# Moving the constants and staging tiles of a float32 trunk kernel in on-chip memory, and starting the shared region at a multiple of 256 bytes

## The chip, the core and the metric

The kernel runs on one core of a Trainium2 chip. The metric is the device time of one execution in microseconds (us). Before the change three runs took 2451.73, 2452.22 and 2452.22 us (median 2452.22). One more execution was profiled: it took 2452.22 us, of which its trace covers 2450.5 us from the first to the last instruction; the remaining 1.7 us lie around the trace.

The engines are TensorE (PE in the profile, its weight loads PEld), VectorE (DVE), ScalarE (ACT), GpSimd (POOL) and SyncE (SP), which here only issues DMAs. On-chip memory (SBUF) has 128 partitions; a tile has the same byte address in each, and "address" below always means that byte address.

## The reference, cut to what matters

A model trunk with 256 tokens and width 2048, all in float32. Layer 0 mixes tokens by retention and RWKV-7, layer 1 by a convolution and a gated linear recurrence; after each comes a squared-ReLU MLP of width 8192, and a final norm ends it.

```python
h = h + even_mixer(rmsnorm(h, ev_norm))            # in: 2048 x 7456, out: 2048 x 2048
h = h + relu(rmsnorm(h, ff_norm[0]) @ ff_w1[0])**2 @ ff_w2[0]   # 2048 x 8192, 8192 x 2048
h = h + odd_mixer(rmsnorm(h, od_norm))             # in: 2048 x 4096, out: 2048 x 2048
h = h + relu(rmsnorm(h, ff_norm[1]) @ ff_w1[1])**2 @ ff_w2[1]
out = rmsnorm(h, final_norm)
```

## The kernel before, in words

**Weights as a stream.** Every large matrix product is cut into groups of 512 output columns (one has 288) and each group into 8 units of 256 rows of the weight matrix. A unit is one DMA of 512 KB into a slot of the ring `raw` (4 slots, issued by SP in `load_unit`). ACT copies it to the rounded form `w_hi` (L189), DVE writes the remainder `w_lo` = `raw` - `w_hi` (L194), and PE multiplies the unit with the activations, which are split in the same way: for each block of 128 rows and each half of the tokens it forms hi x hi, hi x lo and lo x hi (L205 to L207). In these matmuls the 128x128 block of activations is the loaded weight of the array, and 512 columns of `w_hi` or `w_lo` stream past it. There are 95 groups, of which 94 have 512 columns.

**Activations.** The left factor is `xT_hi`, `xT_lo` for products that read the normed input, and `hidA_hi`, `hidA_lo`, `hidB_hi`, `hidB_lo` (together "hid") for the products that read a hidden activation: half of each MLP and both output projections. After a group, ACT takes the result to the staging tile `stg` (L270), POOL squares it in the MLPs (L278), PE transposes it with the identity in `con` (L302), and ACT and DVE split it into hid. Groups of residual columns are added to `x` by DVE (L352).

**RWKV.** Between 180 and 585 us the kernel runs the RWKV recurrence in 8 passes: small float32 matmuls of 128x128 blocks (all issued by the helper at L688) on tiles named `key_bd`, `beta_bd`, `level_a`, `inv_t` and the like, into whose gaps the matmuls of the retention projection are woven.

**What sets the order.** Every engine has its program in a fixed, hand-written order, and semaphores by count tie them together. Nothing in it reads an address to choose an order.

**Memory.** One slab from address 16512 holds everything. `Region` is a bump allocator over it: each call gives the next bytes, rounded up to 32. `lasting` holds what lives through the kernel. A shared region begins at `low`; in it the tiles of RWKV, retention, the odd layer and hid lie over one another, since they live at different times. Before, `lasting` was in two parts: `x`, `xT_hi`, `xT_lo`, `raw`, `w_hi`, `w_lo` ahead of the shared region, then 93568 bytes of shared region, then `par` (gains and biases), `con` (identity, ones, masks), `ssq`, `rstd`, `lam`, `stg` and `junk` behind it.

Of the kernel before, what the change touches and what calls it, by code (L numbers as in the profile page):

```python
# [11 lines left out]
P = 128  # L12
T = 256
HALVES = T // P
D = 2048
KT = D // P
# [34 lines left out]
def trunk(nc, x_in, params, consts, cossin, rdecay, ev_w_in, ev_w_out, rw_w2, rw_a2, rw_g2, od_w_in, gx_w, ga_w,  # L51
          od_w_out, ff_w1, ff_w2, final_norm, out):
    ctx = ExitStack()
    with ctx:
# [17 lines left out]
        slab_start = -(-nc.sbuf_base // 32) * 32  # L72
# [13 lines left out]
        lasting = Region(0)  # L86
# [3 lines left out]
        raw = lasting("raw", [P, RING, KU, WIDE])  # L90
        w_hi = lasting("w_hi", [P, RING, KU, WIDE], F32R)
        w_lo = lasting("w_lo", [P, RING, KU, WIDE], F32R)
        HALF = KT // 2 * T * 4
        low, shared_end = lasting.at, lasting.at + 93568

        lasting = Region(shared_end)
        par = lasting("par", [P, NPAR])
        con = lasting("con", [P, NCONST])
        ssq = lasting("ssq", [P, 4, HALVES])
# [2 lines left out]
        stg = lasting("stg", [P, 2, HALVES, WIDE])  # L102
        junk = lasting("junk", [P, WIDE])
        ident = con[:, CIDENT:CIDENT + P]

        at_a = Region(low)
        hidA_hi, hidA_lo = (at_a(n, [P, KT // 2, T], F32R) for n in ("hidA_hi", "hidA_lo"))
        at_b = Region(low + 4 * HALF)
        hidB_hi, hidB_lo = (at_b(n, [P, KT // 2, T], F32R) for n in ("hidB_hi", "hidB_lo"))
# [32 lines left out]
        gate_a = od_a("gate_a", [P, KT, T])  # L142
        od_b = Region(low + 4 * HALF)
        gate_x = od_b("gate_x", [P, KT, T])
        x_rest = Region(low + 2 * HALF)
        conv = x_rest("conv", [P, KT, T])
# [1633 lines left out]
```

## Time and profile before

| | |
|---|---|
| profiled execution | 2452.22 us |
| its span in the trace | 2450.5 us |
| PE busy | 2403.4 us, 98% of the span |
| PE weight loads busy | 2021.8 us, 83% |
| DVE busy | 1407.3 us, 57% |
| ACT busy | 1133.0 us, 46% |
| POOL busy | 240.3 us, 10% |
| DMA | 411.21 MB, 168 GB/s over the span |
| mean granted PE clock | 0.996 of full speed |

An engine is busy while it carries out an instruction; overlapping matmuls count once. Matmuls are pipelined, so the distance from one start to the next tells more than the duration of one.

### The profile page before, as it was taken

The numbers are of one execution on the slowest core, as the hardware profiler recorded it, in microseconds if no ns is written. First come the engines' busy times: TensorE is split into PE (matmuls) and PEld (weight loads), VectorE is DVE, ScalarE is ACT, GpSimd is POOL, SyncE is SP. The second block draws the span as 40 slices with busy tenths as digits, with TensorE's granted clock in tenths as the row PEclk, the third lists the DMA queues.
The fourth block names the chain that finished last, engine by engine and source line by source line (L and its number), as shares of the span: only waits on it lengthen the run. The fifth ranks groups of instructions, "written<-read, shape, count | busy, mean of one in ns | idle before, by whom it ended". The sixth has DMA issues, their size and how long they took to land.

```text
span 2450.5 us, 32124 instructions
## 1 busy us (share of the span) xinstructions
PE 2403.4 (98%) x11710; PEld 2021.8 (83%) x11710; DVE 1407.3 (57%) x1613; ACT 1133.0 (46%) x1459; POOL 240.3 (10%) x184
## 2 busy tenths in 40 slices
PE   7999999999999999999999999989999999999998
PEld 6878888888788888888888888878888888888886
DVE  5467777775555555545555566775555554555554
ACT  5454444444444444344344545765443443443443
POOL 0001123342000000000000000230000000000001
PEclk9999999999999999999999999999999999999999
DMA  7652223333565666565666565545666656656654
GB/s 219 189 147 84 83 86 88 88 87 97 166 186 180 197 190 186 192 189 182 196 183 192 184 201 177 175 147 186 181 192 194 189 182 196 185 187 196 188 186 158
DMA packets 215432, 411.21 MB, mean 168 GB/s; under 512 B 13264, under 2 KB 19792, under 8 KB 215184
## 3 DMA queue, kind: packets, MB, share of 16 engines
q1 hardware_dynamic: 213888, 407.01, 54.5%
q0 software_dynamic: 1424, 2.49, 0.4%
q8 instruction: 89, 1.46, 0.3%
q14 instruction: 31, 0.25, 0.0%
HBM read 407.35 MB, written 2.10 MB: 167 GB/s over the span
## 4 chain that ended last, share of the span: by engine, by line
PE 87%; DVE 2%; ACT 2%; issue 1%; POOL 0%; ACTq 0%; DVEq 0%; POOLq 0%
PE acc L205 25%; PE acc L207 25%; PE acc L206 25%; PE tp L688 6%; PE tp L302 2%; PE acc L688 1%; PE acc L1490 1%; PE tp L1490 1%; DVE stg L635 1%; ACT w_hi L189 0%; ACT L680 0%; DVE w_lo L194 0%; DVE state L858 0%; DVE gate_t L1553 0%; DVE stg L636 0%
## 5 line engine op out<-in xcount | busy, mean ns | idle before, releaser
L194 DVE TENSOR_TENSOR w_lo<-raw,w_hi 128x1024 fp32r<-128x1024 f32 (+1 forms) x760 | 987.1, 1304 | 891.9 <-ACT w_hi L189 890.2
L189 ACT ACTIVATE w_hi<-raw 128x1024 fp32r<-128x1024 f32 (+1 forms) x760 | 800.4, 1056 | 945.3 <-PE acc L207 933.7
L205 PE MATMUL acc<-w_hi,xT_hi 128*128 128x512 f32 (+1 forms) x1760 | 706.1, 401 | 6.5 <-DVE w_lo L194 4.3
L207 PE MATMUL acc<-w_hi,xT_lo 128*128 128x512 f32 (+1 forms) x1760 | 684.4, 389 | 0.0
L206 PE MATMUL acc<-w_lo,xT_hi 128*128 128x512 f32 (+1 forms) x1760 | 683.5, 388 | 0.0
L205 PEld LDWEIGHTS acc<-w_hi,xT_hi 128*128 128x128 f32 x1760 | 332.1, 189 | 69.0 <-DVE w_lo L194 3.8
L207 PEld LDWEIGHTS acc<-w_hi,xT_lo 128*128 128x128 f32 x1760 | 331.2, 188 | 68.7
L206 PEld LDWEIGHTS acc<-w_lo,xT_hi 128*128 128x128 f32 x1760 | 332.1, 189 | 60.5
L205 PE MATMUL acc<-w_hi,hidA_hi 128*128 128x512 f32 x640 | 252.8, 395 | 6.3 <-DVE hidA_lo L1524 6.3
L206 PE MATMUL acc<-w_lo,hidA_hi 128*128 128x512 f32 x640 | 251.1, 392 | 0.0
L207 PE MATMUL acc<-w_hi,hidA_lo 128*128 128x512 f32 x640 | 250.9, 392 | 0.0
L205 PE MATMUL acc<-w_hi,hidB_hi 128*128 128x512 f32 x640 | 250.6, 392 | 0.0
L207 PE MATMUL acc<-w_hi,hidB_lo 128*128 128x512 f32 x640 | 249.1, 389 | 0.0
L206 PE MATMUL acc<-w_lo,hidB_hi 128*128 128x512 f32 x640 | 249.0, 389 | 0.0
L278 POOL TENSOR_TENSOR stg<-stg 128x1024 f32<-128x1024 f32 x32 | 60.6, 1895 | 1358.3 <-ACT stg L270 1358.3
L205 PEld LDWEIGHTS acc<-w_hi,hidA_hi 128*128 128x128 f32 x640 | 121.5, 190 | 31.6 <-issue 6.7
L207 PEld LDWEIGHTS acc<-w_hi,hidA_lo 128*128 128x128 f32 x640 | 121.3, 190 | 25.5
L206 PEld LDWEIGHTS acc<-w_lo,hidA_hi 128*128 128x128 f32 x640 | 121.5, 190 | 24.8
L207 PEld LDWEIGHTS acc<-w_hi,hidB_lo 128*128 128x128 f32 x640 | 120.1, 188 | 25.0
L205 PEld LDWEIGHTS acc<-w_hi,hidB_hi 128*128 128x128 f32 x640 | 120.1, 188 | 24.7
L206 PEld LDWEIGHTS acc<-w_lo,hidB_hi 128*128 128x128 f32 x640 | 120.2, 188 | 24.7
L270 ACT ACTIVATE stg<-acc,rstd 128x512 f32<-128x512 f32 (+1 forms) x94 | 59.2, 681 | 68.1 <-PE acc L207 67.8
(230 smaller groups left out, 1731.1 us busy)
## 6 DMA issues: line engine op xcount, KB each, us to landing
raw<-in_ff_w SPq DMA_DIRECT2D x512, 512.0 KB, 3.7
raw<-in_ev_w_in SPq DMA_DIRECT2D x112, 512.0 KB, 3.6
raw<-in_od_w_in SPq DMA_DIRECT2D x64, 512.0 KB, 4.1
raw<-in_ev_w_out SPq DMA_DIRECT2D x32, 512.0 KB, 3.8
raw<-in_od_w_out SPq DMA_DIRECT2D x32, 512.0 KB, 3.8
raw<-in_ev_w_in SPq DMA_DIRECT2D x8, 288.0 KB, 5.3
x<-in_x_in SPq DMA_DIRECT2D x4, 512.0 KB, 6.6
gate_w<-in_gx_w SPq DMA_DIRECT2D x8, 256.0 KB, 2.8
```

The costliest lines, as they stand in the source:

```text
L189: act.activation(w_hi[:, j % RING, :, 0:wide], raw[:, j % RING, :, 0:wide], ACT.Copy).then_inc(hi_ready, 1)
L194: dve.tensor_tensor(w_lo[:, j % RING, :, 0:wide], raw[:, j % RING, :, 0:wide], w_hi[:, j % RING, :, 0:wide], ALU.subtract).then_inc(lo_rea ...
L205: nc.tensor.matmul(o, hi[:, tok], wh, start=(kt == 0), stop=False)
L206: nc.tensor.matmul(o, hi[:, tok], wl, start=False, stop=False)
L207: last = nc.tensor.matmul(o, lo[:, tok], wh, start=False, stop=(kt == KT - 1))
L270: last = act.activation(stg[:, g["bank"], h, 0:g["wide"]], acc[2 * g["bank"] + h][:, 0:g["wide"]], g.get("func", ACT.Relu if g["post"] == ...
L278: pool.tensor_tensor(s, s, s, ALU.mult).then_inc(squared, 1)
L302: last = nc.tensor.transpose(tp[2 * b + c // 2][0:s.shape[1], (c % 2) * T + h * P:(c % 2) * T + (h + 1) * P], s, ident)
L635: own(dve.reciprocal(nrm_t, nrm_t))
L688: return nc.tensor.matmul(out, lhsT, rhs, start=first, stop=last)
L1490: last = nc.tensor.matmul(odd_gate_banks(v, n)[i][:, jh * T:(jh + 1) * T], gate_w[:, n % 2, i, ih, jh * P:(jh + 1) * P], conv[:, 2 * n + i ...
```

## The change

The seven tiles `par` to `junk` are allocated right behind `w_lo`, without a gap, and the shared region begins behind them, at the next address that is a multiple of 256. All tiles keep their shapes and their order within their region.

```diff
         w_lo = lasting("w_lo", [P, RING, KU, WIDE], F32R)
-        HALF = KT // 2 * T * 4
-        low, shared_end = lasting.at, lasting.at + 93568
-
-        lasting = Region(shared_end)
         par = lasting("par", [P, NPAR])
         con = lasting("con", [P, NCONST])
...
         junk = lasting("junk", [P, WIDE])
         ident = con[:, CIDENT:CIDENT + P]
-
+        HALF = KT // 2 * T * 4
+
+
+        low = lasting.at + -(slab_start + lasting.at) % (2 * P)
         at_a = Region(low)
```

The addresses that follow, and what is left of each when it is divided by 256:

| tile | before | rest | after | rest |
|---|---|---|---|---|
| `x` | 16512 | 128 | 16512 | 128 |
| `xT_hi`, `xT_lo` | 32896, 49280 | 128 | the same | 128 |
| `raw`, `w_hi`, `w_lo` | 65664, 82048, 98432 | 128 | the same | 128 |
| `par` | 208384 | 0 | 114816 | 128 |
| `con` | 209504 | 96 | 115936 | 224 |
| `stg` | 215840 | 32 | 122272 | 160 |
| `junk` | 224032 | 32 | 130464 | 160 |
| shared region, `hidA_hi`, `gate_a` | 114816 | 128 | 132608 | 0 |
| `hidB_hi`, `z` | 147584 | 128 | 165376 | 0 |
| `v_bd` to `seen_v` (RWKV), `qT` | from 177856 | 192 | from 195648 | 64 |
| `gate_w` | 180544 | 192 | 198336 | 64 |

The seven tiles move down by 93568 bytes and the shared region up by 17792; both are odd multiples of 128, so what is left on division by 128 is the same for every tile. Each engine has the same instructions, with the same shapes and the same waits, in the same order; only addresses in them differ. All line numbers from `HALF` on are lower by up to 4 (those of the engines' work by 1).

## Rows read from the trace of the kernel before

**Rows 1.** The page: span, busy time, granted clock.
```profile
span 2450.5 us, 32124 instructions
PE 2403.4 (98%) x11710; PEld 2021.8 (83%) x11710; DVE 1407.3 (57%) x1613; ACT 1133.0 (46%) x1459; POOL 240.3 (10%) x184
PEclk9999999999999999999999999999999999999999
```

**Rows 2.** The page: the chain that ended last, by engine.
```profile
PE 87%; DVE 2%; ACT 2%; issue 1%; POOL 0%; ACTq 0%; DVEq 0%; POOLq 0%
```

**Rows 3.** Waits of PE, longest first: total us, times, longest.
```profile
PE tp L302 <- DMA par<-in_params: 6.5, 1, 6.5
PE acc L205 <- DVE hidA_lo L1524: 6.3, 1, 6.3
PE tp L1298 <- POOL qT L1203: 4.4, 2, 2.8
PE acc L205 <- DVE w_lo L194: 4.3, 2, 3.4
...
PE tp L688 <- ACT rhs_u L917: 1.5, 7, 0.2
```

**Rows 4.** The last chain by time, 2438 to 2451 us: start, us, what.
```profile
2438.55 0.24 PE acc L207
...
2443.87 1.22 ACT x L1694 x2
```

**Rows 5.** Timeline near 1000 us, left factor hid: start, duration, instruction.
```profile
999.72 0.39 PE L206 MATMUL acc<-w_lo,hidA_hi 128*128 128x512 f32 x1
...
999.95 0.19 PEld L205 LDWEIGHTS acc<-w_hi,hidA_hi 128*128 128x128 f32 x1
...
1000.37 1.06 ACT L189 ACTIVATE w_hi<-raw 128x1024 fp32r<-128x1024 f32 x1 [1.66 <-PE acc L207]
1000.40 0.39 PE L206 MATMUL acc<-w_lo,hidA_hi 128*128 128x512 f32 x1
...
1003.35 0.39 PE L207 MATMUL acc<-w_hi,hidB_lo 128*128 128x512 f32 x1
```

**Rows 6.** Timeline near 1105 us, left factor xT, POOL squaring `stg`.
```profile
1103.93 0.39 PE L205 MATMUL acc<-w_hi,xT_hi 128*128 128x512 f32 x1
...
1104.20 1.90 POOL L278 TENSOR_TENSOR stg<-stg 128x1024 f32<-128x1024 f32 x1 [21.62 <-ACT stg L270]
...
1105.10 2.07 DVE L194 TENSOR_TENSOR w_lo<-raw,w_hi 128x1024 fp32r<-128x1024 f32 x1 [2.73 <-ACT w_hi L189]
...
1105.97 0.39 PE L205 MATMUL acc<-w_hi,xT_hi 128*128 128x512 f32 x1
```

**Rows 7.** Groups by line and shape: busy us, mean ns, idle before.
```profile
L302 PE MATMUL tp<-con,stg 128*128 128x128 f32 x372 | 48.2, 272 | 1.3 <-ACT stg L270 1.3
...
L688 PE MATMUL tp<-beta_bd,key_bd 128*128 128x128 f32 x320 | 42.1, 274 | 0.0
```

**Rows 8.** One line, the convolution taps: duration min, median, max in ns.
```profile
L1471 DVE SCALAR_TENSOR_TENSOR conv<-x_raw,par,conv x48: 473/480/2628, 1456.9 to 1558.2; 128x256 f32<-128x256 f32 x48
```

**Rows 9.** The page: hid as left factor, staging and squaring.
```profile
L206 PE MATMUL acc<-w_lo,hidA_hi 128*128 128x512 f32 x640 | 251.1, 392 | 0.0
L205 PE MATMUL acc<-w_hi,hidB_hi 128*128 128x512 f32 x640 | 250.6, 392 | 0.0
...
L278 POOL TENSOR_TENSOR stg<-stg 128x1024 f32<-128x1024 f32 x32 | 60.6, 1895 | 1358.3 <-ACT stg L270 1358.3
...
L270 ACT ACTIVATE stg<-acc,rstd 128x512 f32<-128x512 f32 (+1 forms) x94 | 59.2, 681 | 68.1 <-PE acc L207 67.8
```

**Rows 10.** DMA issues: count, KB each, median us from issue to landing.
```profile
raw<-in_ff_w SPq DMA_DIRECT2D x512, 512.0 KB, 3.7
...
stg<-in_final_norm SPq DMA_DIRECT2D x1, 1024.0 KB, 6.5
...
par<-in_params SPq DMA_DIRECT2D x1, 137.5 KB, 4.7
```

## The prediction

> **What bounds the kernel now.** I read the totals first, then the chain that ended last, then who PE waited for, and then timelines at two places. The totals show PE busy for 2403.4 of 2450.5 us, at full granted clock in every slice, and no other engine above 57% [rows 1]. So PE sets the time, and 47.1 us are left in which it does nothing. The chain of waits says the same: 87% of it is PE, and the issue gaps, DVE and ACT have 1 to 2% each [rows 2]. Of the 47.1 us, 11.7 come after the last matmul (it ends at 2438.8 us, and the span at 2450.5 [rows 1, 4]) and 6.5 at the very start, where PE waits for the load of `par`; the other 28.9 us are short waits in between, the longest 6.3 us [rows 3].
>
> "PE busy" could still hide slack, because matmuls overlap. The timelines show the real step. Where the left factor is hid, 16 steps take from 999.72 to 1003.35 us, that is 226.9 ns each [rows 5]. Where it is xT, 9 steps take from 1103.93 to 1105.97 us, 226.7 ns each [rows 6]. The 512 columns of one matmul at the upper clock level, 2.4 GHz, need 213.3 ns, so PE is within 13.6 ns of its own floor at each step. A weight load takes 190 ns [rows 5] and fits under the step.
>
> **The change, part by part.** Nothing is added, removed or reordered on any queue; the waits are the same, and so are the DMAs and their sizes. What can cost or save time is the address alone, and only these parts of it change: bit 7 and the bits above. I take the groups of operands in turn.
>
> *The stream of weights.* `raw`, `w_hi`, `w_lo`, `x` and the xT tiles keep their addresses. So all 760 weight loads from memory, ACT's rounding, DVE's remainder and the columns that stream through PE are as before, as are both factors in 55 of the 95 groups. Cost 0.
>
> *Hid as the weight of the array.* This is the largest part that moves: six groups of 640 matmuls (two of them in [rows 9]), 3840 in all, whose left factor starts on a rest of 0 in place of 128 after division by 256. No tile that PE reads in the kernel before starts on a multiple of 256, so the trace has no such matmul, and I bound it. Upper bound of a gain: all 13.6 ns over the column time go, 3840 x 13.6 = 52 us. Upper bound of a loss: the same 13.6 ns more, 52 us. The value that I take is 0, by the nearest rows. First, xT at 32896 and hid at 114816 and 147584 lie far apart and step alike within 0.2 ns [rows 5, 6]. Second, two kinds of small float32 matmul have operands on different rests: the transposes of `stg` with `con` (32 and 96) come to 48.2 / 372 = 130 ns each, and the RWKV products of `beta_bd` and `key_bd` (both 192) to 42.1 / 320 = 132 ns [rows 7]. Third, what moves is the side that is loaded, and at 190 of 227 ns a faster load would not be seen.
>
> *RWKV, retention, odd-layer and `stg` operands of ACT, DVE and POOL.* The convolution taps are the best test in the trace: the rows of `x_raw` are 1036 bytes long and the taps are shifted by 4 bytes, so the 48 instructions start on rests from 128 upward and round past 0 to 60. Their minimum is 473 and their median 480 ns; the maximum of 2628 ns belongs to an instruction that met POOL [rows 8]. A start address that shifts by single words is not seen there. I take 0. As for the bound, these engines reach the end only through PE's 28.9 us of middle waits: if all their moved work became 10% cheaper or dearer, the waits would shrink or grow by about 2.9 us. The tail of 11.7 us has `stg` (final gains) and `junk` in it, and 10% of that is 1.2 us, which I fold into the same bound.
>
> *DMA.* The transfers into moved tiles are single ones (`par`, `con`, the masks, the final gains) or lie under other work; the stream into `raw`, which holds 407 of 411 MB with its neighbours, stays. The only moved transfer that PE visibly waits for is `par`: 4.7 us from issue to landing, 6.5 us of PE wait [rows 3, 10]. I take 0, and 10% of its 4.7 us, 0.5 us, as the bound in either direction.
>
> The Trainium skill speaks against the change here ("DMA: Bandwidth & Descriptors", section "How a descriptor splits into AXI transactions"): a descriptor is cut at 256-byte boundaries, and a start off such a boundary still pays for the bytes below it. `par` goes from a rest of 0 to 128. By that rule its 1100 bytes per partition cost 39 beats of 32 bytes in place of 35; estimated from the page, with the 4.7 us of this trace, that is +0.5 us. No row of the kernel before shows the two starts side by side. The sum above doesn't use it.
>
> **Sum.** 2450.5 us of span + 1.7 us around it + 0 + 0 + 0 + 0 = 2452.2 us. The profiled execution took exactly the median of the three runs, so nothing has to be carried over.
>
> **The rivals.** The measurement can tell a change of about 0.2%, 4.9 us, from none; I use that as the border below.
>
> *A, faster: aligned weights shorten PE's step.* The 13.6 ns over the column time could be the price of handing over to a weight block whose 512-byte rows straddle three 256-byte pieces in place of two. Then the 3840 hid matmuls would each save up to 13.6 ns: 2452.2 - 52 = 2400 us; from 1.3 ns per step on, it would pass the border. For it: the overhead is there and is constant, as a fixed cost would be. Against it: the weight load is hidden, and the small matmuls with rests of 32 and 96 against 192 and 192 show no difference worth the name.
>
> *B, slower: `stg` and `con` now lie directly behind `w_lo`.* If the memory had blocks in which one engine's access holds up another's, PE reading `w_lo` would now collide with ACT writing `stg` (59.2 us in all) and POOL squaring it (60.6 us) [rows 9]. A slowdown of PE by 10% over these 119.8 us gives +12 us, 2464 us; it decides from 4.1% on (4.9 / 119.8). Against it: in [rows 5] ACT writes one slot of `w_hi` while PE reads another slot of the same tile, 4 to 12 KB away, closer than `stg` will be to most of `w_lo`, and PE keeps its 227 ns. In [rows 6] POOL squares `stg` and doubles a DVE subtraction to 2.07 us, and PE still steps by 226.7 ns. The Trainium skill ("SBUF — State Buffer", section "Who interferes with whom") says that only the port pair shared by VectorE and GpSimd causes contention; the trace agrees in these two places, and by it B is worth nothing, and the time stays at 2452.2 us.
>
> *C, small shifts of phase.* If some DVE or ACT work in RWKV or the retention part were touched, the 28.9 us of waits would move: 2449 to 2455 us. That is inside the border for nearly every size I can give it, so I count it with the forecast.
>
> *D, the change does less than it says.* A multiple of 256 for the start of the shared region doesn't give one to each tile in it: the RWKV matrices keep a rest of 64 and `gate_w` too, and `par`, which had a rest of 0, loses it. So even if alignment mattered, part of the RWKV stage would see none. This gives 2452.2 us as well, for another reason.
>
> **How the numbers follow.** Forecast with C and D: 0.88. A: 0.05, and 0.02 for some gain of over 4.9 us in the RWKV and retention waits that I can't price. B: 0.04, and 0.01 for another loss. So faster by over 0.2%: 0.07; within 0.2%: 0.88; slower by over 0.2%: 0.05. The range is that of the forecast, since A and B together hold less than 2 in 10: 2.9 us down and 2.9 + 0.5 us up, 2449.3 to 2455.6 us. Both ends lie within the border.
>
> **What would show it right or wrong.** In the profile after: the step of the hid matmuls again 226 to 228 ns (A wrong) and that of the xT matmuls while POOL squares `stg` too (B wrong); hid matmul groups at 389 to 395 ns in the mean as before; the convolution taps at a median near 480 ns; PE's first wait, for `par`, at 6.5 us, or up to 0.5 us more if the rule on descriptors bites; a last matmul that ends at 2438.8 within 3 us; and the same instruction counts. The prediction is wrong if the hid step leaves 226 to 228 ns, if the middle waits of PE leave 26 to 32 us, or if the span leaves 2447.6 to 2453.9 us.

## The result and the profile after

The changed kernel takes 2472.07 us (median of 6 runs, 2471.53 to 2472.66), the kernel before 2451.78 us (median of 6 runs, 2450.64 to 2452.22). The ratio is 1.0084, with a 95% interval of 1.007 to 1.0096: 20.3 us slower. The prediction was 2452.2 us, range 2449.3 to 2455.6.

The page of the changed kernel, for [rows 1, 2] (span and busy time, granted clock, chain by engine):

```profile
span 2471.6 us, 32124 instructions
PE 2425.5 (98%) x11710; PEld 2024.6 (82%) x11710; DVE 1411.0 (57%) x1613; ACT 1132.6 (46%) x1459; POOL 239.2 (10%) x184
PEclk9999999999999999999999999999999999999999
...
PE 88%; DVE 2%; ACT 2%; issue 1%; POOL 0%; ACTq 0%; DVEq 0%; POOLq 0%
```

The span grew by 21.1 us and PE's busy time by 22.1 us. PE is idle for 46.1 us where it was 47.1. So the time went into matmuls and into no wait, and the clock is the same (0.995 of full speed in the mean, 0.996 before). The waits of PE (total us, times, longest), for [rows 3]:

```profile
PE tp L301 <- DMA par<-in_params: 6.5, 1, 6.5
PE acc L204 <- DVE hidA_lo L1523: 6.3, 1, 6.3
PE acc L204 <- DVE w_lo L193: 4.3, 2, 3.4
PE tp L1297 <- POOL qT L1202: 4.2, 2, 2.7
```

Which matmuls is told by the page's groups (busy us, mean ns), for [rows 9]:

```profile
L204 PE MATMUL acc<-w_hi,xT_hi 128*128 128x512 f32 (+1 forms) x1760 | 706.3, 401 | 5.8 <-DVE w_lo L193 4.3
...
L204 PE MATMUL acc<-w_hi,hidA_hi 128*128 128x512 f32 x640 | 256.2, 400 | 6.3 <-DVE hidA_lo L1523 6.3
L205 PE MATMUL acc<-w_lo,hidA_hi 128*128 128x512 f32 x640 | 254.5, 398 | 0.0
L206 PE MATMUL acc<-w_hi,hidA_lo 128*128 128x512 f32 x640 | 254.1, 397 | 0.0
L204 PE MATMUL acc<-w_hi,hidB_hi 128*128 128x512 f32 x640 | 254.0, 397 | 0.0
L206 PE MATMUL acc<-w_hi,hidB_lo 128*128 128x512 f32 x640 | 252.6, 395 | 0.0
L205 PE MATMUL acc<-w_lo,hidB_hi 128*128 128x512 f32 x640 | 252.5, 395 | 0.0
```

The six hid groups add up to 1523.9 us, against 1503.5 us on the page of before: +20.4 us, which is the change. The largest xT group went from 706.1 to 706.3 us. The hid matmuls are spread from 585 us to the last one at 2459.8 us, so no slice of the page's time bars shows it.

The timeline of the changed kernel near 1004 us (start, duration), for [rows 5]. From 1004.21 to 1007.70 us are 15 steps:

```profile
1004.21 0.39 PE L205 MATMUL acc<-w_lo,hidA_hi 128*128 128x512 f32 x1
1004.22 0.19 PEld L206 LDWEIGHTS acc<-w_hi,hidA_lo 128*128 128x128 f32 x1
1004.45 0.39 PE L206 MATMUL acc<-w_hi,hidA_lo 128*128 128x512 f32 x1
...
1005.14 0.40 PE L206 MATMUL acc<-w_hi,hidA_lo 128*128 128x512 f32 x1
...
1005.38 0.40 PE L204 MATMUL acc<-w_hi,hidA_hi 128*128 128x512 f32 x1
...
1006.76 0.40 PE L204 MATMUL acc<-w_hi,hidA_hi 128*128 128x512 f32 x1
...
1007.00 0.40 PE L205 MATMUL acc<-w_lo,hidA_hi 128*128 128x512 f32 x1
...
1007.70 0.39 PE L205 MATMUL acc<-w_lo,hidB_hi 128*128 128x512 f32 x1
```

That is 232.7 ns per step in place of 226.9. The steps aren't alike. By the trace's starts in ns, seven lengths repeat: 231, 232, 228, 230, 233, 241 and 232 ns (93% of the hid steps equal the one seven steps later within 1 ns). The matmuls repeat by threes, so the long step falls on each kind in turn: above, from an L206 to an L204 at 1005.14, and seven steps later from an L204 to an L205 at 1006.76. Whether another engine is at work makes little difference: the hid steps during which ACT, DVE and POOL are all idle (242 of them) take 232.6 ns in the mean, those beside ACT alone 232.3 and beside DVE alone 232.4. The weight loads still take 0.19 us. Below, "the step" of a tile is the mean distance between the starts of neighbouring large matmuls with that left factor, over its whole trace, steps over 300 ns (a gap) left out. For hid it went from 226.8 to 232.4 ns, and 3840 x 5.6 ns is 21.5 us. For xT, where I take the steps from the `w_hi` to the `w_lo` matmul with `xT_hi`, it stayed at 227.0 (227.1 after).

### The profile page after: what moved, and what is told of

Read it like the earlier page. It is cut to its first block, busy times and chain, and to the rows that moved or that the text cites. A ratio compares the mean times of both kernels' runs of the same rounds, so it can differ in the third digit from the quotient of the medians.

```text
span 2471.6 us, 32124 instructions
## 1 busy us (share of the span) xinstructions
PE 2425.5 (98%) x11710; PEld 2024.6 (82%) x11710; DVE 1411.0 (57%) x1613; ACT 1132.6 (46%) x1459; POOL 239.2 (10%) x184
## 4 chain that ended last, share of the span: by engine, by line
PE 88%; DVE 2%; ACT 2%; issue 1%; POOL 0%; ACTq 0%; DVEq 0%; POOLq 0%
PE acc L204 26%; PE acc L206 25%; PE acc L205 25%; PE tp L687 6%; PE tp L301 2%; PE acc L687 1%; PE acc L1489 1%; PE tp L1489 1%; DVE stg L634 0%; ACT w_hi L188 0%; ACT L679 0%; DVE w_lo L193 0%; DVE state L857 0%; DVE gate_t L1552 0%; DVE stg L635 0%
## 5 line engine op out<-in xcount | busy, mean ns | idle before, releaser
L204 PE MATMUL acc<-w_hi,xT_hi 128*128 128x512 f32 (+1 forms) x1760 | 706.3, 401 | 5.8 <-DVE w_lo L193 4.3
L206 PE MATMUL acc<-w_hi,xT_lo 128*128 128x512 f32 (+1 forms) x1760 | 684.7, 389 | 0.0
L205 PE MATMUL acc<-w_lo,xT_hi 128*128 128x512 f32 (+1 forms) x1760 | 683.9, 389 | 0.0
L204 PEld LDWEIGHTS acc<-w_hi,xT_hi 128*128 128x128 f32 x1760 | 332.1, 189 | 68.5 <-DVE w_lo L193 4.3
L206 PEld LDWEIGHTS acc<-w_hi,xT_lo 128*128 128x128 f32 x1760 | 331.1, 188 | 68.6
L205 PEld LDWEIGHTS acc<-w_lo,xT_hi 128*128 128x128 f32 x1760 | 332.2, 189 | 60.8
L204 PE MATMUL acc<-w_hi,hidA_hi 128*128 128x512 f32 x640 | 256.2, 400 | 6.3 <-DVE hidA_lo L1523 6.3
L205 PE MATMUL acc<-w_lo,hidA_hi 128*128 128x512 f32 x640 | 254.5, 398 | 0.0
L206 PE MATMUL acc<-w_hi,hidA_lo 128*128 128x512 f32 x640 | 254.1, 397 | 0.0
L204 PE MATMUL acc<-w_hi,hidB_hi 128*128 128x512 f32 x640 | 254.0, 397 | 0.0
L206 PE MATMUL acc<-w_hi,hidB_lo 128*128 128x512 f32 x640 | 252.6, 395 | 0.0
L205 PE MATMUL acc<-w_lo,hidB_hi 128*128 128x512 f32 x640 | 252.5, 395 | 0.0
L204 PEld LDWEIGHTS acc<-w_hi,hidA_hi 128*128 128x128 f32 x640 | 121.8, 190 | 34.5 <-issue 6.7
L206 PEld LDWEIGHTS acc<-w_hi,hidA_lo 128*128 128x128 f32 x640 | 121.8, 190 | 28.8
L205 PEld LDWEIGHTS acc<-w_lo,hidA_hi 128*128 128x128 f32 x640 | 122.0, 191 | 27.7
L206 PEld LDWEIGHTS acc<-w_hi,hidB_lo 128*128 128x128 f32 x640 | 120.6, 188 | 28.2
L204 PEld LDWEIGHTS acc<-w_hi,hidB_hi 128*128 128x128 f32 x640 | 120.6, 188 | 27.8
L205 PEld LDWEIGHTS acc<-w_lo,hidB_hi 128*128 128x128 f32 x640 | 120.6, 188 | 27.8
```

The source lines that it names most:

```text
L204: nc.tensor.matmul(o, hi[:, tok], wh, start=(kt == 0), stop=False)
L205: nc.tensor.matmul(o, hi[:, tok], wl, start=False, stop=False)
L206: last = nc.tensor.matmul(o, lo[:, tok], wh, start=False, stop=(kt == KT - 1))
```

## The experiments

Each kernel differs from the changed kernel, or once from the kernel before, in addresses alone. Every ratio is to the kernel before, run beside it (medians of 2449.79 to 2450.97 us). The "rest" is an address modulo 256. `xT_hi`, `xT_lo`, `raw`, `w_hi` and `w_lo` have rest 128 unless told otherwise.

In all but the second, `low` is written as a multiple of 512 plus an offset, and the second half of the shared region gets its own start `low_b`, so that hidA and hidB can be moved apart (A and B are the two offsets; the other tiles that began with the second half begin at `low_b` too, cut here):

```diff
-        low = lasting.at + -(slab_start + lasting.at) % (2 * P)
+        low = lasting.at + -(slab_start + lasting.at) % 512 + A
+        low_b = low + 4 * HALF + (B - A)
...
-        at_b = Region(low + 4 * HALF)
+        at_b = Region(low_b)
...
```

**1. The new place, the old rest** (A = B = 128).

> The changed layout with the shared region 128 bytes further up: hid starts on a rest of 128 (mod 256) again, as the ring and xT do, but stays at its new place behind stg. Theory R (what is left of the address of hid on division by 256 sets the step of its matmuls): the hid step returns from 232.4 to 226.8 ns, time about 2452 us. Rival L (the new place or the new neighbours con and stg are to blame): the hid step stays at 232.4 ns, time about 2472 us.

Measured: 2450.36 us, ratio 1.0000 (0.9991 to 1.001). Hid step 226.8 ns. The place and the neighbours don't matter, to within 0.1% of the time.

**2. The old place, the new rest.** In the kernel before:

```diff
-        low, shared_end = lasting.at, lasting.at + 93568
+        low, shared_end = lasting.at + 128, lasting.at + 93568 + 128
```

> The kernel before, with the shared region and all behind it 128 bytes further up, order of the tiles unchanged: hid at the low place on a rest of 0. Theory R: hid step 232.4 ns, about 2472 us. Rival L: hid step 226.8 ns, about 2452 us.

Measured: 2472.88 us, ratio 1.0093 (1.0077 to 1.011). Hid step 232.4 ns, with `con` and `stg` as far from `w_lo` as ever. 128 bytes alone make the whole difference, at the old place. The group in its trace, against 250.6 in [rows 9]:

```profile
L205 PE MATMUL acc<-w_hi,hidB_hi 128*128 128x512 f32 x640 | 254.0, 397 | 0.0
```

**3. All operands on rest 0** (`lasting` starts at 128, A = B = 256).

> The changed layout with everything 128 bytes up and the shared region a multiple of 512 from the ring: x, xT, ring and hid all start on a rest of 0 (mod 256). Theory R1 (a loaded weight block that starts on a rest of 0 is slow by itself): hid and xT steps both 232.4 ns, 9120 x 5.6 = 51 us over before, about 2503 us. Theory R2 (only the distance between the loaded block and the streamed columns counts; a multiple of 256 is good): both 226.8 ns, about 2452 us.

Measured: 2449.92 us, ratio 0.9999 (0.9989 to 1.0008). Its timeline near 1004 us, hid as left factor:

```profile
1003.94 0.39 PE L207 MATMUL acc<-w_lo,hidB_hi 128*128 128x512 f32 x1
...
1006.20 0.39 PE L208 MATMUL acc<-w_hi,hidB_lo 128*128 128x512 f32 x1
```

Ten steps in 2.26 us, 226 ns each, with hid on the very rest that was slow in the changed kernel. So rest 0 of hid is not bad in itself.

**4. Ring and hid on rest 0, xT on 128** (A = B = 256).

```diff
+        lasting.at += 128
         raw = lasting("raw", [P, RING, KU, WIDE])
```

> Ring and hid on a rest of 0, xT left on 128. R1 (own rest of the weight block): hid step 232.4, xT step 226.8 ns, about 2472 us. R2 (distance between weight block and streamed columns): hid step 226.8, xT step 232.4 ns; 55 groups x 96 matmuls less the narrow one, about 5200 x 5.6 = 29 us over before if the woven RWKV part shows it in full, about 2475 to 2481 us. The steps by left factor in the trace tell, not the total.

Measured: 2473.76 us, ratio 1.0098 (1.0081 to 1.0115). The hid step is 226.9 ns, and now the xT step is long, 232.4 ns, though xT never moved. Its timeline near 1075 us, xT as left factor:

```profile
1074.89 0.39 PE L209 MATMUL acc<-w_hi,xT_lo 128*128 128x512 f32 x1
1075.12 0.40 PE L207 MATMUL acc<-w_hi,xT_hi 128*128 128x512 f32 x1
...
1077.45 0.39 PE L208 MATMUL acc<-w_lo,xT_hi 128*128 128x512 f32 x1
```

Eleven steps in 2.56 us, 233 ns each. The price, 23.5 us, is under the 29 us that the count of the matmuls gives, because many xT matmuls are woven between the small ones of RWKV: of the 5184 xT matmuls of 512 columns, 4730 are followed by another within 300 ns, and over all of these the step went from 227.2 to 232.4 ns, which is 24.6 us. Runs 1 to 4 settle the first question: what counts is whether the loaded blocks and the streamed columns have the same rest, and not which rest it is.

**5 to 8. Other distances** (one profiled execution each; A and B are 128 + the distance).

> Ring and xT as before, hidA 32 and hidB 64 bytes past a multiple of 512 from the ring. Theory S (step: the two 128-byte halves of a 256-byte piece count, so up to 96 is good): both steps 226.8 ns, about 2450 us. Theory T (the cost grows with the distance to the nearest multiple of 256, 5.6 ns at 128): hidA 228.2, hidB 229.6 ns, 1920 x (1.4 + 2.8) = 8 us, about 2458 us. Theory G (some distance is better than 0): a step below 226 ns in one of them, down to the 213.3 ns of the columns.

> hidA 96, hidB 160 bytes past a multiple of 512 from the ring. S: hidA 226.8, hidB 232.4 ns, 1920 x 5.6 = 11 us, about 2461 us. T: both 231.0 ns, 16 us, about 2466 us. G: one below 226 ns.

> hidA 192, hidB 224 bytes past a multiple of 512 from the ring. S: both 232.4 ns, about 2472 us. T: hidA 229.6, hidB 228.2 ns, about 2458 us. G: one below 226 ns.

> hidA 256, hidB 384 bytes past a multiple of 512 from the ring. If the period is 256: hidA 226.8, hidB 232.4 ns, about 2461 us. If it is 512: hidA off its best too (232 ns or more), about 2472 us or more.

Measured: 2474.61, 2477.92, 2467.89 and 2461.68 us, beside 2451.44 us for the kernel before. The steps:

| distance to the ring | 0 | 32 | 64 | 96 | 128 | 160 | 192 | 224 | 256 | 384 |
|---|---|---|---|---|---|---|---|---|---|---|
| step, ns | 226.8 | 233.2 | 233.4 | 234.2 | 232.4 | 233.6 | 229.0 | 233.3 | 226.9 | 232.4 |

The groups of the kernel with distances 256 (hidA) and 384 (hidB):

```profile
L207 PE MATMUL acc<-w_lo,hidB_hi 128*128 128x512 f32 x640 | 252.3, 394 | 0.0
...
L207 PE MATMUL acc<-w_lo,hidA_hi 128*128 128x512 f32 x640 | 250.6, 392 | 0.0
```

256 is as good as 0, and 384 costs what 128 costs, so the period divides 256; and since 128 is bad, it isn't 128. Theories S and T are both wrong: 32 bytes already cost 6.4 ns, and the cost doesn't rise with the distance. Theory G is wrong too: no distance beats 0. Distance 192 is the cheapest of the bad ones, which I can't explain. The kernel's allocator rounds to 32 bytes, and no finer start was tried. Each distance but 0 and 128 rests on a single trace.

**9. xT_lo alone on rest 0.** 128 bytes of padding ahead of `xT_lo`, and 128 more ahead of `raw`; from here on A = B = 128.

> xT_lo alone on a rest of 0, all other factors and the ring on 128, the shared region a multiple of 512 from the ring. The block of xT_lo is loaded while the columns of w_lo stream (the hi x lo matmul before it) and is used with w_hi in the next. Theory N (a load conflicts with the stream that runs while it loads): of the three steps of each part only the one from the w_lo matmul to the xT_lo matmul is long, 232.4 ns, the two others 226.8. Rival O (a block's distance to the columns that it is then multiplied with counts): the step from the xT_lo matmul to the next is long. Either way a third of what moving the ring against xT cost: 23.5 / 3 = 8 us, about 2458 us. Rival P (one late load shifts all that follows): all three steps lengthen.

Measured: 2468.49 us, ratio 1.0076 (1.006 to 1.0093). The time was missed by 10 us. Its timeline near 1072 us, with the loads:

```profile
1072.22 0.40 PE L209 MATMUL acc<-w_lo,xT_hi 128*128 128x512 f32 x1
1072.23 0.19 PEld L210 LDWEIGHTS acc<-w_hi,xT_lo 128*128 128x128 f32 x1
1072.46 0.40 PE L210 MATMUL acc<-w_hi,xT_lo 128*128 128x512 f32 x1
1072.46 0.19 PEld L208 LDWEIGHTS acc<-w_hi,xT_hi 128*128 128x128 f32 x1
1072.69 0.39 PE L208 MATMUL acc<-w_hi,xT_hi 128*128 128x512 f32 x1
...
1072.92 0.40 PE L209 MATMUL acc<-w_lo,xT_hi 128*128 128x512 f32 x1
```

In the mean over the trace the step in which `xT_lo` is loaded takes 232.4 ns, the next one, in which it is in use and `xT_hi` is loaded, 233.9 ns, and the third 227.1 ns. Neither N nor O alone gives two long steps, and P, all three, is wrong.

**10. raw alone on rest 0.** DMA writes it, ACT and DVE read it; PE doesn't. Padding of 128 bytes ahead of `raw` and ahead of `w_hi`.

> Only raw, which DMA writes and ACT and DVE read but PE never reads, on a rest of 0; every operand of the large matmuls on 128. Theory PE (only PE's own two reads are in conflict): all steps 226.8 ns, about 2450 us, same as before. Rival M (the traffic of DMA, ACT and DVE through the ring takes part): steps above 227 ns, up to 9120 x 5.6 = 51 us more.

Measured: 2450.01 us, ratio 1.0002 (0.9993 to 1.0012), hid step 226.8 ns, xT step 227.0. The rest of `raw`, and with it of the DMA's writes, doesn't matter, as theory PE has it.

**11. w_lo alone on rest 0.** Padding ahead of `w_lo` and ahead of `par`.

> w_lo alone on a rest of 0, all loaded blocks and w_hi on 128. In the run with xT_lo moved, two of three steps were long: the one in which the moved block was loaded (stream w_lo) and the next, in which it was in use (stream w_hi, next block at distance 0). Theory U (a block with a distance costs while it loads and while it is in use): here only the step of the w_lo stream has distances, so one of three steps is long, 5.6 to 7 ns x 3040 = 17 to 21 us, about 2467 to 2471 us. Theory V (a disturbed step leaves the next one out of step as well, whatever its addresses): two of three long, 13.7 ns x 3040 = 42 us, about 2490 us. In both the step from the xT_hi, w_hi matmul to the w_lo matmul stays at 226 to 227 ns.

Measured: 2486.25 us, ratio 1.0145 (1.0128 to 1.0162). For hidA the step from the `w_hi` to the `w_lo` matmul takes 230.9 ns, the next 229.6 and the third 233.0, all long: U (one) and V (two) are both wrong. The first of them runs with every address in it, of the stream, the block in use and the block being loaded, at distance 0. It is so with xT too (231.3 ns); here it runs from 1104.67 to 1104.91 us:

```profile
1104.67 0.40 PE L208 MATMUL acc<-w_hi,xT_hi 128*128 128x512 f32 x1
1104.67 0.19 PEld L209 LDWEIGHTS acc<-w_lo,xT_hi 128*128 128x128 f32 x1
1104.91 0.40 PE L209 MATMUL acc<-w_lo,xT_hi 128*128 128x512 f32 x1
...
1105.14 0.39 PE L210 MATMUL acc<-w_hi,xT_lo 128*128 128x512 f32 x1
```

One odd tile of the four that PE reads in a group (`w_hi`, `w_lo` and the two parts of the left factor) costs 35 us, more than the change under study.

**12. xT_lo and w_lo on rest 0.** Both paddings.

> xT_lo and w_lo both on a rest of 0, everything else on 128. Now each block is loaded while columns at distance 0 stream (xT_lo during w_lo, xT_hi during w_hi), while the pairs that are multiplied with each other lie 128 apart in two of three cases. Theory N (only the load and the stream that run at the same time count): all xT steps 226.8 ns, hid steps as with w_lo alone moved (about 231), so about 1280 x 13 = 17 us over before, 2467 us. Theory W (what counts is also the change of rest from one stream or load to the next): xT steps above 228 ns, about 2480 us or more.

Measured: 2486.53 us, ratio 1.0145 (1.0128 to 1.0162). Its timeline near 1110 us, xT as left factor:

```profile
1110.28 0.40 PE L210 MATMUL acc<-w_hi,xT_hi 128*128 128x512 f32 x1
1110.28 0.19 PEld L211 LDWEIGHTS acc<-w_lo,xT_hi 128*128 128x128 f32 x1
...
1110.52 0.40 PE L211 MATMUL acc<-w_lo,xT_hi 128*128 128x512 f32 x1
1110.52 0.19 PEld L212 LDWEIGHTS acc<-w_hi,xT_lo 128*128 128x128 f32 x1
1110.75 0.40 PE L212 MATMUL acc<-w_hi,xT_lo 128*128 128x512 f32 x1
...
1110.98 0.39 PE L210 MATMUL acc<-w_hi,xT_hi 128*128 128x512 f32 x1
1110.99 0.19 PEld L211 LDWEIGHTS acc<-w_lo,xT_hi 128*128 128x128 f32 x1
...
1111.21 0.39 PE L211 MATMUL acc<-w_lo,xT_hi 128*128 128x512 f32 x1
```

Steps of 0.24, 0.23 and 0.23 us, then 0.23, in spite of distance 0 between each load and the stream beside it: theory N is wrong, and W, which only said that the xT steps would be above 228 ns, holds as far as it goes (they are 230.8, 230.2 and 232.4 ns in the mean, by kind).

No version beat the kernel before. Runs 1, 3 and 10 equal it, and in each of them all tiles that PE's large matmuls read have one rest.

## Why the prediction was wrong, point by point

**What bounds the kernel** was right: PE, at its own step, and nothing beside it. The tail after the last matmul (11.8 us both times), the first wait for `par` (6.5 us both times) and the middle waits (27.8 us; 28.9 in the prediction) hardly moved, so "sum of the other parts 0" held. That takes in rival C. The convolution taps (min, median, max in ns) are as in [rows 8]:

```profile
L1470 DVE SCALAR_TENSOR_TENSOR conv<-x_raw,par,conv x48: 472/480/2626, 1467.0 to 1568.4; 128x256 f32<-128x256 f32 x48
```

**The stream of weights, "cost 0"**: right for the 55 xT groups, for a reason that I hadn't seen: xT kept its distance to the ring.

**Hid as the weight of the array** is the step that failed. I bounded it at 52 us on either side, took 0, and it is +20.4 us on the page. The signs that I had named say the same: the hid step left 226 to 228 ns (232.4), the hid groups have means of 395 to 400 ns, and the last matmul ends at 2459.8 us and not near 2438.8. Three arguments led there, and each is answered by a run.

- "xT and hid lie far apart and step alike." They did, but xT, hidA, hidB and the ring all had rest 128. I had the column of rests in front of me and asked whether a row had rest 0; I didn't ask whether any row had *two different* rests among the operands of one large matmul. None had. Runs 3 and 4 show that this is the quantity that counts.
- "Small float32 matmuls have operands on different rests and cost alike." True, but those two rows compare only two distances between the loaded and the streamed side, 192 (`stg` to `con`) and 0 (`beta_bd` to `key_bd`), which no run changed; so that they cost the same after the change says nothing. Others did change their distance, and the statement stands with them: the transposes of `ret_tok` with `con` take 109 ns from start to start at distances 0, 32, 96, 160 and 192 (runs 6, before, 7, 1 and 5), and the 256-column products of `conv` and `gate_w` 216 ns at 0, 64, 192 and 224 (runs 6, 8, before and 5). But the two forms of matmul aren't comparable: the small float32 matmuls take 109 ns for 128 columns, 0.85 ns each, while the large ones pass a column in 227 / 512 = 0.44 ns. What lengthens the steps of the fast stream left the slow one alone; why is not shown.
- "What moves is the loaded side, and at 190 of 227 ns a faster load would not be seen." The load does stay hidden and at 0.19 us. It is the step of the stream that lengthens.

**The range** failed by the same step. I had written the bound of 52 us and then built the range from the other terms, as if the two rivals were the only ways to reach that bound. A term with 3840 repeats and no row that tests it should have kept a part of its bound in the range.

**Rival A** (aligned weights shorten the step, 2400 us) didn't come; run 3 shows that with everything aligned to 256 the step is what it was, so the 13.6 ns over the column time aren't a cost of rest 128.

**Rival B** had the sign, and not the mechanism. Run 2 is slow with `stg` and `con` far away, and run 1 fast with them at the new place. The rule of the Trainium skill that I weighed there ("SBUF — State Buffer", section "Who interferes with whom") lists the two read ports of TensorE as independent and says that it never waits on anyone. For two different engines these traces agree: the hid step is the same beside ACT, beside DVE and beside neither (232.3, 232.4 and 232.6 ns in the changed kernel). For TensorE's own two reads they don't: the mean step depends on the distance between them, by up to 7.4 ns. One reading in that argument was off: the subtraction of [rows 6] took 2.07 us where the median of its kind is 1.23, which is two thirds more and not double.

**Rival D** had the time of the forecast and fell with it; the cost came through hid, which did get its multiple of 256. (180544 and 198336, the starts of `gate_w`, leave 64 and 192, not 192 and 64 as the table of addresses has it; no sum uses them.)

**The rule on descriptors** ("DMA: Bandwidth & Descriptors", section "How a descriptor splits into AXI transactions"), by which the load of `par` would take 0.5 us more, isn't seen: PE's first wait is 6.5 us in both traces, and the load took 4.6 us from issue to landing after 4.7. It wasn't a fair test either: the section speaks of bytes that a transaction reads, and the change moved only the side to which `par` is written.

**What stays open.** Which of PE's reads disturb each other inside a step. The load and the stream beside it don't suffice (run 9, second step, and run 12), the block in use and its stream don't either (run 9, first step), and the two together don't (run 11, the step of 230.9 ns). Nor does a step's length follow from its own addresses: in the changed kernel the same kind of step takes from 228 to 241 ns, in a cycle of seven, so an explanation has to reach over several steps. Why the cycle has seven steps is open too. That it is a matter of PE's own reads is shown as far as the addresses of `raw`, `con`, `stg` and the place of hid have been ruled out. ACT's and DVE's traffic through `w_hi` and `w_lo` moved along with PE's stream in every run; no run separates them, but the steps are as long while both engines are idle.

## What to carry to other kernels

In a stream of large matmuls that is bound by PE's own step, give all tiles that it reads, loaded blocks and streamed columns alike, the same address modulo 256; here a factor, or one tile, off by 32 bytes or more cost 2 to 7 ns per step of 227 in the mean, and up to 1.45% of the kernel. (A distance of 256 was as good as 0 in the one run that had it.) Before a layout is changed, write down not only each tile's address but the differences between operands of one instruction, and ask which rows have tested them. If every row of the trace has the same value of something, the trace says nothing about it, and its bound belongs in the range.

## What the runs showed of the hardware that I had not expected

- The mean step of float32r matmuls of 512 columns with a fresh 128x128 block each depends on the distance of the two operands modulo 256: 226.8 ns at 0, 229.0 at 192, and 232.4 to 234.2 at 32, 64, 96, 128, 160 and 224. The place in memory, 17 KB higher or lower, has no effect (runs 1 and 2).
- The slow case is no constant: in the changed kernel the hid steps go through a cycle of seven from 228 to 241 ns, which runs across the cycle of three matmuls and goes on while the other engines are idle.
- Float32 matmuls of 128 and 256 columns kept their step, 109 and 216 ns, at the five and four distances that occurred for them.
